# Four DRAM fills moved behind the convolution's square and the attention's last values in a two-layer encoder step

## The reference, cut to what matters

```
mod  = silu(c) @ w_ada + b_ada                    # shift, scale, gate for both sub-layers
h    = rms_norm(x) * (1 + scale) + shift
proj = h @ w_in                                   # q, k, v, index q, index k, index weights, u
attn = top-k sparse attention; the index scores sum relu(iq . ik) * iw pick the keys
g    = a * sigmoid(b)                             # a, b are the halves of u
y    = silu(layer_norm(causal_depthwise_conv(g, width 31) + conv_b))
x    = x + gate * (concat(attn, y) @ w_out)
x    = x + gate * moe(norm(x))                    # 16 experts, each token goes to two
```

## Time and profile before

| | |
|---|---|
| median of 3 runs | 1345.04 us (1344.86 to 1347.79) |
| profiled execution | 1352.91 us, its span 1351.1 us |
| PE, DVE, ACT, POOL busy | 88%, 44%, 24%, 11% of the span |
| mean DMA rate | 210 GB/s; 283.96 MB in all |
| four fills | 16.8 MB of the 42.50 MB of POOL's DMA queue |

### The profile page before, as it was taken

The page is one execution under the profiler, slowest core; times in us unless marked ns, Lnnn a source line. Parts: engine busy times, 40 slices in busy tenths (PEclk is TensorE's granted clock), DMA queues, the critical chain, the costliest instruction groups (busy, mean ns, idle before and its releaser), DMA issues.

```text
span 1351.1 us, 16307 instructions
## 1 busy us (share of the span) xinstructions
PE 1187.3 (88%) x6331; PEld 714.7 (53%) x6331; DVE 590.0 (44%) x1492; ACT 325.4 (24%) x765; POOL 153.8 (11%) x218
## 2 busy tenths in 40 slices
PE   4898996997999898999962999999789989999990
PEld 0463353553445586777741554555454568777760
DVE  1326897205446631111114537896465663111115
ACT  2214210024532111111112433201475111111111
POOL 0312140101000151000002004300100010000002
PEclk9999997997999899999985989999899989999995
DMA  9518999281770479999938030223330055999976
GB/s 361 169 63 311 392 338 284 59 290 51 248 291 32 160 207 382 369 361 369 352 144 304 26 104 9 72 78 104 104 80 8 32 182 184 324 360 368 364 248 226
DMA packets 136887, 283.96 MB, mean 210 GB/s; under 512 B 11581, under 2 KB 91877, under 8 KB 130409
## 3 DMA queue, kind: packets, MB, share of 16 engines
q1 hardware_dynamic: 113056, 203.46, 44.4%
q0 software_dynamic: 8352, 42.50, 9.1%
q10 hardware_dynamic: 15401, 36.94, 8.2%
HBM read 236.86 MB, written 52.40 MB: 214 GB/s over the span
## 4 chain that ended last, share of the span: by engine, by line
PE 75%; DVE 9%; DMA 8%; ACT 3%; issue 2%; SPq 2%; POOLq 0%; POOL 0%; ACTq 0%; DVEq 0%
PE ps L517 46%; PE ps L865 7%; PE ps L540 6%; PE ps L709 5%; PE ps L769 2%; PE ps L560 2%; DMA X<-in_x_sample 2%; PE ps L826 2%; PE ps L917 2%; DMA W<-in_w_up 2%; PE ps L529 1%; SPq L428 1%; DMA arena<-y_d,sid 1%; DMA arena<-arena 1%; DMA arena<-in_w_down 1%
## 5 line engine op out<-in xcount | busy, mean ns | idle before, releaser
L517 PE MATMUL ps<-W,arena 128*128 128x256 f32 (+1 forms) x1280 | 347.2, 427 | 9.7 <-DMA W<-in_w_up 5.2
L517 PEld LDWEIGHTS ps<-W,arena 128*128 128x128 f32 x1280 | 241.7, 193 | 84.4 <-issue 49.3
L517 PE MATMUL ps<-W,hT 128*128 128x512 f32 (+1 forms) x384 | 156.0, 563 | 3.1 <-ACT hT L1073 3.1
L540 PE MATMUL ps<-C,arena 128*128 128x128 f32 (+3 forms) x795 | 111.8, 278 | 47.6 <-DVE arena L1497 18.1
L540 PEld LDWEIGHTS ps<-C,arena 128*128 128x128 f32 (+3 forms) x795 | 90.6, 143 | 88.3 <-issue 37.9
L865 PE MATMUL ps<-W,hT 128*128 128x512 f32 (+1 forms) x384 | 130.8, 541 | 0.3 <-DMA W<-in_w_out 0.3
L517 PE MATMUL ps<-hT,W 128*128 128x128 f32 (+1 forms) x512 | 126.6, 408 | 0.0
L517 PEld LDWEIGHTS ps<-W,hT 128*128 128x128 f32 x384 | 74.1, 197 | 77.3 <-issue 62.6
L1908 DVE TENSOR_TENSOR arena<-arena,ps 128x256 f32<-128x256 f32 x32 | 13.5, 421 | 219.3 <-ACT arena L1372 211.6
L517 PEld LDWEIGHTS ps<-hT,W 128*128 128x128 f32 x512 | 77.8, 191 | 49.6 <-issue 49.2
L865 PEld LDWEIGHTS ps<-W,hT 128*128 128x128 f32 (+1 forms) x384 | 57.3, 178 | 62.4 <-issue 59.3
(11 more groups left out here) (267 smaller groups left out, 1188.0 us busy)
## 6 DMA issues: line engine op xcount, KB each, us to landing
W<-in_w_ada SPq DMA_DIRECT2D x48, 1024.0 KB, 7.1
W<-in_w_gate SPq DMA_DIRECT2D x32, 1024.0 KB, 10.5
W<-in_w_up SPq DMA_DIRECT2D x32, 1024.0 KB, 12.8
W<-in_w_down SPq DMA_DIRECT2D x32, 1024.0 KB, 7.7
y_d<-arena ACTq DMA_DIRECT2D x33, 512.0 KB, 7.3
W<-in_w_in SPq DMA_DIRECT2D x16, 1024.0 KB, 9.2
arena<-x_d SPq DMA_DIRECT2D x31, 512.0 KB, 11.7
W<-in_w_out SPq DMA_DIRECT2D x8, 1024.0 KB, 7.6
```

Of the source, the lines that this page charges most:

```text
L517: ins = T.matmul(out, l, r, start=n == 0, stop=n == len(pairs) - 1, skip_group_check=True)
L540: count(T.transpose(o, i, ident[0:m, 0:m]), done if n == len(outs_ins) - 1 else None)
```

## The change

The wait for the last index score product and the four fills behind it are taken from their place in POOL's queue, ahead of the query norms. Two fills are now issued, with no wait of their own, behind the square of the convolution output. The other two come behind a wait for the copies of eight of the nine attention groups. All four still come before the scatters.

```diff
@@ POOL's queue, layer loop @@
                     norm_qk(G, chain, r, t0, t1, KH)
                     rope(pool, G, qkr, r, t0, t1, KH, route[:, 512:768], L["pch"], n_chain, L["ropeq"], n + 1)
-                if l == 0:
-                    pool.wait_ge(L["rel"], len(SCORES))
-                    for n in range(3):
-                        pool.dma_start(x_d[n * D:n * D + D, :], A["w_out"][0]).then_inc(s_fill, 16)
-                    pool.dma_start(y_d[XROW:SPARE, :], A["w_out"][0]).then_inc(s_fill, 16)
                 for n, t in enumerate(ATTN):
                     pool.wait_ge(L["qinv"], n + 2)
...
                 pool.wait_ge(L["lnx"], 1)
                 G.tensor_tensor(sqc[:, :, :], cy[:, :, :], cy[:, :, :], ALU.mult).then_inc(L["lnsq"], 1)
+                if l == 0:
+                    for n in range(2):
+                        pool.dma_start(x_d[n * D:n * D + D, :], A["w_out"][0]).then_inc(s_fill, 16)
+                    pool.wait_ge(L["on"], len(GROUPS) - 1)
+                    pool.dma_start(x_d[2 * D:3 * D, :], A["w_out"][0]).then_inc(s_fill, 16)
+                    pool.dma_start(y_d[XROW:SPARE, :], A["w_out"][0]).then_inc(s_fill, 16)
```

## The result

The changed kernel takes 1354.52 us (median of six runs, 1352.52 to 1364.39) where the kernel before takes 1345.53 beside it: ratio 1.0077, 95% interval 1.0051 to 1.0104, so slower by 9 us in the medians and 10 us by the ratio (7 to 14). Two more comparisons gave 1.0095 (1.0061 to 1.0129) and 1.0086 (1.0056 to 1.0116). The profiled execution took 1353.04 us, span 1351.2, which is no slower than the profile of before.

The account below looks back on a forecast made before the run. PE, busy 88% of the span, was taken as the bound, so transfers count only where PE waits. -14.6 + 0 + 20.2 = +5.6 us on the median 1345.04 gave 1350.7, say 1351, range 1338 to 1360.

Parts of the forecast that it names:

- The gain, -14.6: At conv(0) of layer 0: without fills at 150 us, PE's 12.4 us wait on shifted copies and 2.2 us slow start go.
- Fills 1 and 2, 0: Fills issued at 312 us delay modulation weight loads, which land by 345, 15 us before PE's step: cost 0.
- Fills 3 and 4, +20.2: At the output products: fills hold the fourth output-weight load; PE waits 18.0 us, plus a 2.2 us slow start.
- first data of the fills: 385.7 + 4.2 = 389.9: Fills 3 and 4: issue at 385.7 plus 4.2 us lag, with the third output-weight load (landing 390.4) nearly through.
- inside the same wait: Output products: third load, six turns late, lands at 407; three products more make 417.7, within the fourth load's 18.0 us wait.
- rival 3: Third output load caught too: PE stands from 390.5 to as late as 416.9; +14.0 us, 1359 us; chance 18%.
- One packet per turn: DMA queues alternate packet by packet; during fills each engine lets another queue pass one small packet per 2.9 us.
- rival 1: Output weights get through, as fill data starts late or queues pass many packets a turn; -14.6, 1330 us; chance 16%.
- rival 2: Fourth output load partly through, under nine packets left on the slowest engine; wait 3 to 14 us, 1333 to 1347; chance 16%.
- rival 4: The wait at conv(0) stays because something other than the fills makes it; +20.2 alone, 1365 us; chance 2%.
- What would show it: Signs: no conv(0) wait; output-weight wait beginning near 386, lasting 15 to 20 us; fourth load landing 30 us or more after issue.
- the signs I had named for being wrong: Fourth output load landing in under 20 us, the wait beginning at the third load, or modulation weights coming late.

Follow-up runs that it names:

- e3: Changed kernel with fills 3 and 4 in the same place, each split into two column halves (smaller packets); 1327.9 us, ratio 0.9897 to the kernel before.
- e2: Changed kernel with fills 3 and 4 waiting for the first finished output product instead of the eighth attention copy; 1331.04 us, ratio 0.9909 to the kernel before.
- e1: Changed kernel run again with a profile, no edit; 1354.24 us, ratio 1.0095 to the kernel before.
- e9: Changed kernel run again with a profile, no edit; 1360.78 us, ratio 1.0086 to the kernel before.
- e10: Changed kernel run again for one look, no edit; 1357.27 us in one run.
- e12: Kernel before run again for one look, no edit; 1346.56 us in one run.
- e11: Kernel before against itself with a profile, no edit; ratio 0.9986.
- e7: Kernel before with its four fills still at 150 us, each split into two column halves; 1339.57 us, ratio 0.9948 to the kernel before.

## Why the prediction came out as it did

The forecast was 1351.0 in a range of 1338 to 1360, slower with 61%; it is 1354.5 and slower. The sign and the mechanism held, and one term was too small.

- *The gain, -14.6.* Right: A fell by 14.2 us in the mean of three and four profiles, and the wait on shifted copies is gone. A little luck is in it. The wait taken away is 11.0 us in the mean (10.3 to 12.4), and the slow start 2.0, not 2.2: PE's timeline has 7.94 us for `conv(1)`, of which the chain in the earlier trace rows shows the last 7.76. That is 13.0; the other 1.2 us come from slower matmuls later in A in two of the three profiles of before, shown below, and the sum did not have them.
- *Fills 1 and 2, 0.* Right: the late loads landed 10 us before their use.
- *Fills 3 and 4, +20.2.* The mechanism is right (e3, e2), the size is not: +22.8 in the mean, and it comes in another shape. The step that was mis-sized is "first data of the fills: 385.7 + 4.2 = 389.9", with the third load "nearly through", five or six packets short of its end. On the new clock that is 373.2, and the DMA records of the profile after have the first fill packet at 372.60: the issue came at 368.70, 0.3 us earlier than 385.7 - 16.7, and the lag was 3.9 us, not 4.2. The loads for their part ran 0.4 us behind that clock: their first 1536 packets, as many as three loads have, had ended at 372.04, where before it was 388.35. The third load landed 2.05 us after that mark in before (390.4), so at that pace it would have landed at 374.1, an estimate: 1.5 us after the fills' first packet instead of 0.5. It was caught.

  PE's wait gives two turns in e1, six in the first profile and all eight in e9 and e10. Up to six turns are the case of my own sum, which put the third load at 407 "inside the same wait": 391.26 + 16.7 is 408, and the cost of both executions was 19.1 us against 20.2. All eight are rival 3 with its 18%, and cost 26.5 us. The changed kernel does one or the other from one execution to the next, and +22.8 is the mean of two and two; with a margin of 0.4 us between them I should have given them about equal chances. Halfway between the forecast's +5.6 and rival 3's +14.0 is +9.8.
- *One packet per turn*, against the rule that would have given rival 1: right in all profiles, and shown by e3. A packet of a fill is 64 KB and not 57; the 127 of the earlier trace rows have a few tiny ones among them. Two fills are then eight turns of 3.2 us for each engine instead of nine of 2.9, which makes no difference to the sum. Rivals 1, 2 and 4 did not come.
- *What would show it.* The fourth load took 34.7 us, over the 30 given. But the wait began at 373.55, at the third load, and not at 386; that is one of the signs I had named for being wrong. It was badly chosen, since my own sum let the third load be late.

Within A, the three profiles of before lie 2.3, 2.4 and -1.1 us from 189.6 us plus their wait at `conv(0)` and its slow start of 2.0 us. PE's timeline shows where the first two lose it. Before, then e12:

```profile
318.77 6.30 PE L517 MATMUL ps<-arena,C 128*128 128x512 f32 x16
339.50 3.55 PE L560 MATMUL ps<-W,scT 128*32 128x512 f32 x16
```

```profile
320.17 4.54 PE L517 MATMUL ps<-arena,C 128*128 128x512 f32 x16
339.12 1.92 PE L560 MATMUL ps<-W,scT 128*32 128x512 f32 x16
```

From 339.5 to 343.0 the granted clock was 0.53 before, the lower level, and 1.00 in e12 in the same work; e11 is like before (6.33 and 3.57 us).

What stays open: why the clock was low there in two executions of three; which DMA engine was the slowest; and why the third load had more packets left in some executions. In e1, where PE waited least, 1768 packets of the output loads had started when the fills' data came, in e10, where it waited longest, 1561. But e9 with 1690 waited longer than the first profile with 1659, so the count over all engines doesn't settle it.

## What to carry to other kernels

Before you move a large transfer to another place, look at the size of its packets: the DRAM to DRAM copy of contiguous rows ran here in packets of 64 KB, and while it lasted it left every other queue about one small packet per turn. Split it into smaller rows (e3, e7), or issue it behind the landing of what the critical engine needs next (e2); either gave back what the move had cost. The best versions here, e3 at ratio 0.9897 and e2 at 0.9909, keep the moved fills and beat both kernels. And where a cost depends on which of two transfers ends first, by less than a microsecond, several profiles are needed: the first pair of profiles alone, 1352.91 and 1353.04 us, shows a change that costs nothing, and four executions of one program showed waits of 14.1, 17.7, 24.5 and 25.1 us in the same place.

## What the runs showed of the hardware

Splitting the copies cost little: in e3 the fills moved 4.18 MB in 16 us from 374 to 390 beside 1.43 MB of weights, where the large packets moved 7.34 MB in 24 us with 0.34 MB beside them. GpSimd's DMA issue to landing for 4 MB was 15.1 us with the queues empty (e2) and 16.6 to 17.8 us with loads in them. What grows is the time to first data: in the DMA records the first packet starts 1.2 to 1.3 us after the issue in e2 and for the first two fills of the changed kernel, and 3.8 to 4.0 us after it where loads were under way (the third fill of the changed kernel in all four profiles, and the first fill at 150 us in before, e11 and e12).

The large packets hold up the issuing of DMAs too. SP's timeline, before and after:

```profile
387.70 1.98 SPq L406 DMA_DIRECT2D W<-in_w_up  x1
371.00 26.10 SPq L406 DMA_DIRECT2D W<-in_w_up  x1
```

PE's later waits for the `w_gate` and `w_up` weights are alike, 5.7 us before and 5.5 after.
